# Gate projection of one TensorE pass less: both halves of the gate weights in one loaded tile, the result rows added on GpSimd

## What is computed

```python
h = rms_norm(x, norm_mix_g[l])
p = h @ w_in[l]                      # columns: q_a, k_a, v_a, o_a, i_a (8), f_a (8), q_b, ...
i_pre = i_a.astype(jnp.float32) + b_if[l, :H_A].astype(jnp.float32)
f_pre = f_a.astype(jnp.float32) + b_if[l, H_A:].astype(jnp.float32)
logf = jax.nn.log_sigmoid(gate(f_pre))
b = jnp.cumsum(logf, axis=-1)        # then used with i_pre for the decays of the mLSTM heads
```

## Time and profile before

| | |
|---|---|
| median of 3 runs | 1224.93 us (1224.92 to 1225.07) |
| span of the profiled execution, first to last instruction | 1223.2 us |
| own time of the profiled execution | not recorded apart; the median stands 1.7 us above the span |
| TensorE busy / weight loads | 99% / 81% |
| VectorE, ScalarE, GpSimd busy | 64%, 52%, 6% |
| chain that ended last | 92% TensorE, 7% VectorE, 1% ScalarE |
| the gate tile's 24 matmuls | 13.79 to 19.35 us |
| transposes that read `g_out` | from 30.60 us |

### The profile page before, as it was taken

One profiled execution on the slowest core, in us unless ns is written; L12 is line 12 of the kernel. 1 busy time (PEld: TensorE's weight loads), 2 busy tenths in 40 slices (PEclk: granted clock), 3 DMA queues, 4 the chain that ended last, 5 costly groups with the idle time before them and its releaser, 6 DMA issues.

```text
span 1223.2 us, 15539 instructions
## 1 busy us (share of the span) xinstructions
PE 1214.1 (99%) x5820; PEld 990.4 (81%) x5820; DVE 782.1 (64%) x1224; ACT 638.1 (52%) x928; POOL 72.9 (6%) x149
## 2 busy tenths in 40 slices
PE   8999999999999999999999999999999999999998
PEld 7888888888888888888888888888877777777887
DVE  7736543783565366569377474697679989656671
ACT  7645544663554463554444353565566556566720
POOL 2101110210111021000000000000000000000000
PEclk9999999999999999999999999999999999999999
DMA  5421322323132236314215224115213333635621
GB/s 214 137 86 37 112 69 77 103 77 103 43 112 69 78 103 213 117 35 141 100 35 199 76 79 161 35 53 206 93 46 125 132 115 112 233 104 181 241 70 69
DMA packets 25622, 134.21 MB, mean 110 GB/s; under 512 B 3352, under 2 KB 3528, under 8 KB 12768
## 3 DMA queue, kind: packets, MB, share of 16 engines
q1 hardware_dynamic: 16224, 107.14, 25.4%
q0 software_dynamic: 4736, 16.90, 3.9%
q10 hardware_dynamic: 4608, 9.44, 2.0%
HBM read 121.92 MB, written 11.55 MB: 109 GB/s over the span
## 4 chain that ended last, share of the span: by engine, by line
PE 92%; DVE 7%; issue 1%; ACT 1%; POOL 0%; DVEq 0%; POOLq 0%; ACTq 0%
PE proj L316 64%; PE proj L1892 7%; PE pm L1892 3%; PE pa L1892 3%; PE pm L1797 2%; PE pa L1808 1%; DVE w_lo L289 1%; PE pa L2087 1%; PE pa L1769 1%; PE pm L1779 1%; DVE idx L1513 1%; PE proj L1818 1%; PE pa L1818 1%; PE pa L2067 1%; PE pa L1788 1%
## 5 line engine op out<-in xcount | busy, mean ns | idle before, releaser
L316 PE MATMUL proj<-h_hi,w_hi 128*128 128x512 f32 (+1 forms) x840 | 328.7, 391 | 0.0
L316 PE MATMUL proj<-h_hi,w_lo 128*128 128x512 f32 (+1 forms) x840 | 323.8, 386 | 0.0
L316 PE MATMUL proj<-h_lo,w_hi 128*128 128x512 f32 (+1 forms) x840 | 323.6, 385 | 0.0
L289 DVE TENSOR_TENSOR w_lo<-w_raw,w_hi 128x2048 fp32r<-128x2048 f32 x84 | 191.5, 2289 | 52.6 <-ACT w_hi L283 52.2
L283 ACT ACTIVATE w_hi<-w_raw 128x2048 fp32r<-128x2048 f32 x84 | 159.9, 1913 | 70.0 <-PE proj L1892 44.2
L316 PEld LDWEIGHTS proj<-h_hi,w_hi 128*128 128x128 f32 x840 | 157.8, 188 | 35.4 <-issue 5.0
L316 PEld LDWEIGHTS proj<-h_hi,w_lo 128*128 128x128 f32 x840 | 157.8, 188 | 32.1
L316 PEld LDWEIGHTS proj<-h_lo,w_hi 128*128 128x128 f32 x840 | 157.9, 188 | 31.4 <-issue 1.0
L316 PE MATMUL proj<-w_hi,h_hi 128*128 128x512 f32 (+1 forms) x288 | 112.8, 391 | 0.4 <-issue 0.4
L316 PE MATMUL proj<-w_lo,h_hi 128*128 128x512 f32 (+1 forms) x288 | 111.7, 388 | 0.0
L316 PE MATMUL proj<-w_hi,h_lo 128*128 128x512 f32 (+1 forms) x288 | 111.5, 387 | 0.0
(11 more groups left out here) (459 smaller groups left out, 2094.6 us busy)
## 6 DMA issues: line engine op xcount, KB each, us to landing
w_raw<-in_wall SPq DMA_DIRECT2D x92, 1024.0 KB, 5.0
b<-in_wall SPq DMA_DIRECT2D x8, 1024.0 KB, 6.0
gates<-gate_st ACTq DMA_DIRECT2D x24, 256.0 KB, 2.0
m_all<-gates POOLq DMA_DIRECT2D x2, 1280.0 KB, 6.9
x_res<-in_x ACTq DMA_DIRECT2D x4, 512.0 KB, 5.0
bc<-gate_rows POOLq DMA_DIRECT2D x8, 256.0 KB, 3.5
x_res<-in_x POOLq DMA_DIRECT2D x4, 512.0 KB, 4.2
x<-x_res POOLq DMA_DIRECT2D x2, 1024.0 KB, 4.5
```

The source lines that it names most:

```text
L289: nc.vector.tensor_tensor(w_lo[:, slot, 4 * half:4 * half + 4, :], w_raw[:, half], w_hi[:, slot, 4 * half:4 * half + 4, :], ALU.subtract)\
L316: mm = nc.tensor.matmul(proj[:, bank, 0:cols] if tokens else proj[:, bank, toks], lhsT, rhs, start=(k == 0 and q == 0), stop=(k == kts - 1 ...
```

## The change

The weight tile `wg_both` holds the rounded columns in 0 to 63 (`wg_hi` in the first 40) and the low ones in 64 to 127 (`wg_lo` in 64 to 103). One matmul with h_hi gives wg_hi·h_hi in result rows 0 to 39 and wg_lo·h_hi in rows 64 to 103. The second pass with h_lo uses the same tile, so that it also adds wg_lo·h_lo, which the kernel before left out. There are 8 matmuls per pass, 16 in all. ScalarE evacuates four groups of 8 rows: f with its bias and its low rows (into `g_G`, free at this time), i and its low rows (into `g_m`). GpSimd adds each pair, and ScalarE's Abs waits for the first add, VectorE's first row operation for the second. GpSimd writes two zero fills of 8x24 columns in place of two of 8x88.

```diff
-        wg_hi = at("wg_hi", 4 * K, [P, KT, P], F32R)
-        wg_lo = at("wg_lo", 8 * K, [P, KT, P], F32R)
+        wg_both = at("wg_both", 4 * K, [P, KT, P], F32R)
+        wg_hi, wg_lo = wg_both[:, :, 0:GATE_COLS], wg_both[:, :, P // 2:P // 2 + GATE_COLS]
...
+            gp.memset(wg_zero[:, :], 0.0).then_inc(S["gate_pool"], 1)
+            gp.wait_ge(S["gate_pool"], 1)
+            for c in (0, P // 2):
+                gp.tensor_copy(wg_both[:, :, c + GATE_COLS:c + P // 2],
+                               wg_zero[:, None, GATE_COLS:P // 2].broadcast_to([P, KT, P // 2 - GATE_COLS]))\
+                    .then_inc(S["gate_pool"], 1)
...
+            for i, (row, r) in enumerate(((g_f, g_G), (g_i, g_m))):
+                gp.wait_ge(S["rows_act"], i + 1)
+                gp.wait_ge(S["tile_free"], i + 1)
+                gp.tensor_tensor(row[:, :], row[:, :], r[:, :], ALU.add).then_inc(S["gate_pool"], 1)
...
-            a.activation(g_i[:, :], proj[0:HEADS, 1], ACT.Identity, bias=bif[:, 0:1]).then_inc(S["tile_free"], 1)
-            a.activation(g_f[:, :], proj[32:32 + HEADS, 1], ACT.Identity, bias=bif[:, 1:2]).then_inc(S["tile_free"], 1)
-            a.wait_ge(S["tile_free"], 2)
+            a.activation(g_f[:, :], proj[32:32 + HEADS, 1], ACT.Identity, bias=bif[:, 1:2]).then_inc(S["rows_act"], 1)
+            a.activation(g_G[:, :], proj[96:96 + HEADS, 1], ACT.Copy).then_inc(S["tile_free"], 1)
+            a.activation(g_i[:, :], proj[0:HEADS, 1], ACT.Identity, bias=bif[:, 0:1]).then_inc(S["rows_act"], 1)
+            a.activation(g_m[:, :], proj[64:64 + HEADS, 1], ACT.Copy).then_inc(S["tile_free"], 1)
+            a.wait_ge(S["gate_pool"], 4)
             a.activation(g_abs[:, :], g_f[:, :], ACT.Abs).then_inc(S["rows_act"], 1)
...
-            v.wait_ge(S["rows_act"], 3)
+            v.wait_ge(S["rows_act"], 5)
+            v.wait_ge(S["gate_pool"], 5)
             v.scalar_tensor_tensor(g_ls[:, :], g_f[:, :], 0.0, g_abs[:, :], ALU.min, ALU.subtract).then_inc(S["rows_dve"], 1)
...
-            t_.wait_ge(S["wg_zero"], 3)
+            t_.wait_ge(S["gate_pool"], 3)
             t_.wait_ge(S["norm_lo"], 1)
             for i, k in enumerate(NORM_ORDER):
                 t_.wait_ge(S["norm_hi"], i + 1)
-                for w in (wg_hi, wg_lo):
-                    t_.matmul(proj[:, 1], w[:, k, :], h_hi[:, k, :], start=(i == 0 and w is wg_hi), stop=False)
+                t_.matmul(proj[:, 1], wg_both[:, k, :], h_hi[:, k, :], start=(i == 0), stop=False)
             for i, k in enumerate(NORM_ORDER):
                 t_.wait_ge(S["norm_lo"], i + 1)
-                mm = t_.matmul(proj[:, 1], wg_hi[:, k, :], h_lo[:, k, :], start=False, stop=(i == KT - 1))
+                mm = t_.matmul(proj[:, 1], wg_both[:, k, :], h_lo[:, k, :], start=False, stop=(i == KT - 1))
```

## The result

The changed kernel takes 1226.15 us (median of 20 runs, 1225.92 to 1227.82), the kernel before 1224.87 us (20 runs, 1224.72 to 1225.14). The ratio is 1.0015 with a 95% interval of 1.0009 to 1.0020. By the medians it is 1.28 us slower, 0.10%, which lies within the 0.2% that the prediction took as no change.

A forecast was written before the change was run, and what follows sets the result against it. TensorE, busy 99%, bounds the kernel; the held-up add delays the gate rows, so its g_out transposes come 1.3 us later, swallowing the 0.34 us gain: 1224.93 + 1.3 = 1226.2 us, range 1224.7 to 1227.3.

The forecast's parts named there:

- The gate tile (0.34 us): TensorE's gate matmuls, 24 to 16: next tile starts 0.34 us earlier, not 1.81, since ScalarE paces the first pass.
- The hand-over to TensorE: Signal travel from another engine to a waiting TensorE, taken as about 0.25 us from the gate tile's start.
- The evacuation costs nothing on TensorE: ScalarE's four evacuations instead of two: Abs at 22.9 us by this alone, but the bank wait costs TensorE nothing.
- the line before L675 has 0.18 us of slack: Evacuation, Abs, row operations and exponential before the g_out transposes: 0.18 us to spare before TensorE waits.
- The add: First GpSimd add of two 512-element rows: 1.05 us, bounds 0.61 and 1.79 us.
- It is held by L289 to its end: First GpSimd add stands still until VectorE's two-input SBUF subtraction ends at 23.11 us, and is over at 24.16.
- Rival (a): GpSimd's add isn't held up by VectorE: 1224.9 us, spread 1224.6 to 1225.5; chance 0.22.
- Abs at 24.26, TensorE at 31.89: Gate rows: Abs 2.70 us later, so TensorE takes up the g_out transposes at 31.89 instead of 30.60, 1.3 us later.
- The 0.34 us vanish in the wait: TensorE's gain from the shorter gate tile is lost in its wait before the g_out transposes.
- The VectorE work behind it has 1 us of cover: w_lo and squares' low parts queued on VectorE end by 37.3 us, TensorE asks at about 38.2: no further cost.
- Rival (c), the clock: TensorE's clock falls after the thin first pass or the idle time at 30.3 us: +2.6, 1227.5 us; chance 0.06.
- The 5.8 us: Assumed length of TensorE's lower clock, from early transposes 0.21 us apart; its matmuls would lose 2.9 us.

The follow-up runs named there:

- e1: Changed kernel with both GpSimd adds left out, so the low weights' part is missing in the gate rows: 1224.55 us.
- e4: Changed kernel with the gate rows' transposes moved behind TensorE's next tile and VectorE's second low part of squares ahead of a w_lo: 1224.60 us.
- e10: Changed kernel with each GpSimd add replaced by a zero fill of the low rows, which only writes: 1224.45 us.
- the copy measured: Changed kernel with each GpSimd add replaced by a copy of the f (i) rows over the low rows: 1225.17 us.
- the cut: Changed kernel with VectorE's second w_lo subtraction of the first group cut into four of 128x512, TensorE waiting slice by slice: 1225.86 us.

## Why the prediction was right, step by step

The forecast was 1226.2 us, the median is 1226.15, and the mechanism is the forecast one. Not all of its terms were, and errors met. That the median agrees to 0.05 us is luck: forecast was +1.3, the lower group has +1.19, and the median of 20 lies at its upper edge only because 8 runs are in the upper group. With three more of the 20 there, it would have been about 1227.5, above the range.

- *The gate tile (0.34 us).* Measured 0.41 in the trace and 0.31 to 0.36 in the times of the kernels that leave out or pass by the wait (e1, e4, e10). ScalarE does pace the first pass: the weight loads start at 14.51, 15.09, 15.67, 16.25 and 16.83 us, 0.58 apart. The hand-over to TensorE was sized too long, 0.25 us; it is some 0.06 (L683 ends at 31.68, L1755 starts at 31.74). The 0.25 read at the gate tile's start contains something else.
- *The evacuation costs nothing on TensorE.* Shown by the kernel without the add. The remark that the line before L675 has 0.18 us of slack was wrong: up to the last row operation it has about 1.2 us, since L675 stood behind ScalarE's own work. The sum didn't use the 0.18. It moved L1129 by 2.70 us and set L675 behind it, as the trace has it.
- *The add.* Taken as 1.05 us with bounds of 0.61 and 1.79; it takes 1.28 alone, and it ended 1.14 us after L289, since part of it lies in the waiting time. The row of the contiguous cast was right for one input (0.61 by its rate, 0.60 for the copy measured); the second input cost 0.68 us more and not 0.44. The Trainium skill, "GPSIMD Engine Reference", section "Elementwise — side-by-side cycle accounting", gives the price from which I had estimated 1.12 us; the trace has 1.28 for the whole instruction.
- *It is held by L289 to its end.* Shown three times over: by 2.46 against 1.28 us for one instruction, by the cut, and by fill against copy. Rival (a) is out. Its price was good: with nothing held, e1 and e10 took 1224.55 and 1224.45 us, where (a) had 1224.6 at the low end. The masks in the trace of before told it three times and not once: four of them from 125.76, 234.03 and 342.31 us took 3.1 us, each time beside L289.
- *Abs at 24.26, TensorE at 31.89.* Measured 24.36 and 31.74. The larger add and the shorter hand-over cancel: 0.1 us too much on the one side, 0.2 too little on the other.
- *The 0.34 us vanish in the wait.* Shown by the eight matmuls put back: 1225.97.
- *The VectorE work behind it has 1 us of cover.* It ended at 37.16 and TensorE wanted it at about 38.1; no wait shows.
- *Rival (c), the clock.* Given 0.06, it came in 12 of 31 runs, so it was priced far too low. Its place was the other one of the two that the text named, the idle time before the transposes and not the thin pass, and it lasted some 3.3 us and not 5.8. That its time of 1227.5 us is close to the upper group is luck: it had 2.9 us lost before the transposes with the wait covering a part, and measured are 1.58 us lost behind them, on top of the whole wait. From the windows of the kernel before, an idle 1.1 us without a fall, I had concluded that idle time of this size is safe. A single execution can't tell that. The 5.8 us were read from transposes 0.21 us apart; the granted clock in that stretch is 1.00, so no row shows the lower level there.

## What to carry to other kernels

Price a GpSimd operation by what VectorE runs at that moment: here what read SBUF beside a two-input VectorE instruction got through only when that one ended, so a longer VectorE instruction is a longer delay. Before fewer instructions are counted as a gain, look for the first wait behind them: here eight matmuls were worth 0.3 us without a wait and nothing with one, and moving the reader behind the next tile (1224.60 us against 1224.91 before) brought them back. The new gap of 1.3 us on TensorE cost its length in every run and a further 1.6 us in 12 of 31, so look at the distribution of the times and not at the median alone.

## What the runs showed of the hardware

- A GpSimd add of 8x512 fp32 takes 1.28 us alone, a copy 0.60 us, a fill 0.52 us. Beside a VectorE subtraction of 128x2048 the add took 2.46 us, the copy 1.79, the fill still 0.52.
- VectorE pays as well: a piece of 128x512, 0.69 us alone, took 1.79 us behind a GpSimd add.
- TensorE's granted clock fell to about half (1.2 of 2.4 GHz) for some 3.3 us after an idle time of about 1.3 us, in the one trace of the upper group. By the times it does so in 12 of 31 executions of this kernel. The fall came at about 33.2 us, when work had begun again at 31.68, and the price was 1.58 us.
- In 3 of 9 traces the clock also fell within a stretch in which TensorE never idled for over 0.4 us at a time (one matmul per 0.58 us, from 13.7 to 17 us), behind an idle 1.26 us. It was 0.51 to 0.64 from 15.5 to 19.5 us, and the gate tile took 1 us more. The same idle time with the dense pass behind it was followed by no fall in the 4 traces that have it.
